# One change at the edges of six stages and in the attention of a two-block kernel

## The reference, cut to what matters

```python
def rwkv_bidir(...):
    kk = k * per_head(k_k)
    kk = kk / jnp.maximum(jnp.sqrt(jnp.sum(kk * kk, axis=-1, keepdims=True)), 1e-12)
    tw = jnp.tanh(xw.astype(f32))
    ...
def banded_attention(q, k, v, max_dist, sinks=None):
    s = ... q k^T * d ** -0.5, masked
    m = max(s.max(axis=-1), sinks)
    p = jnp.exp(s - m[..., None])
    l = p.sum(axis=-1) + jnp.exp(sinks - m)
    o = p @ v
    o = o / l[..., None]
def second_block(...):
    hdn = rmsnorm_2(x, norm_gain)
    ... q, k, v and gates g from hdn @ w_in, norm and rope on q and k
    mixed = concat(o_a * silu(g_a), o_b * silu(g_b))
    return x + mixed @ w_out
```

## Time and profile before

| | |
|---|---|
| median of 3 runs | 2458.24 us (2458.22 to 2469.73) |
| the profiled execution | 2450.08 us, its span 2448.3 us |
| PE busy, its weight loads | 2129.4 us (87%), 1686.8 us (69%) |
| DVE, ACT, POOL busy | 1654.9 (68%), 1268.3 (52%), 675.0 us (28%) |
| mean granted clock of PE | 0.944 of 2.4 GHz |

### The profile page before, as it was taken

The page is one execution under the profiler, slowest core; times in us unless marked ns, Lnnn a source line. Parts: engine busy times, 40 slices in busy tenths (PEclk is TensorE's granted clock), DMA queues, the critical chain, the costliest instruction groups (busy, mean ns, idle before and its releaser), DMA issues. The chain is left out here.

```text
span 2448.3 us, 50472 instructions
## 1 busy us (share of the span) xinstructions
PE 2129.4 (87%) x21006; PEld 1686.8 (69%) x21006; DVE 1654.9 (68%) x2541; ACT 1268.3 (52%) x2327; POOL 675.0 (28%) x472
## 2 busy tenths in 40 slices
PE   5999998499999988973999999999479899778889
PEld 3777787477888743862788888887367788444567
DVE  3665555698888646236899999997367366477941
ACT  5412121476666654434788888886344443365430
POOL 0000011466666501204123322330254545000011
PEclk8999999699999998986999999999799999898999
DMA  7222233333222167326899999997353643200032
GB/s 273 65 56 72 60 83 70 79 68 68 68 69 69 42 225 267 124 113 234 292 394 385 385 388 395 389 386 266 114 190 112 203 111 95 110 1 1 1 104 78
DMA packets 163488, 398.29 MB, mean 163 GB/s; under 512 B 13231, under 2 KB 57405, under 8 KB 163261
## 3 DMA queue, kind: packets, MB, share of 16 engines
q1 hardware_dynamic: 148220, 345.23, 40.3%
q0 software_dynamic: 12224, 44.57, 6.8%
q10 hardware_dynamic: 2816, 5.26, 0.6%
HBM read 348.35 MB, written 46.66 MB: 161 GB/s over the span
## 5 line engine op out<-in xcount | busy, mean ns | idle before, releaser
L1900 DVE TENSOR_TENSOR exp_w_lo<-exp_w,exp_w_hi 128x2048 fp32r<-128x2048 f32 x186 | 414.4, 2290 | 21.9 <-ACT exp_w_hi L1857 21.7
L1857 ACT ACTIVATE exp_w_hi<-exp_w 128x1024 fp32r<-128x1024 f32 x384 | 377.3, 1052 | 66.9 <-PE bank L1819 51.7
L2091 POOL TENSOR_TENSOR w_lo<-mixT,w_hi 128x512 fp32r<-128x512 f32 (+1 forms) x112 | 153.5, 1395 | 175.7 <-ACT w_hi L2167 173.5
L1819 PE MATMUL bank<-exp_w_hi,xsT_lo 128*128 128x512 f32 x512 | 160.8, 396 | 5.7 <-DVE xsT_lo L1904 5.7
L1819 PE MATMUL bank<-exp_w_lo,xsT_hi 128*128 128x512 f32 x512 | 158.8, 392 | 0.0
L1819 PE MATMUL bank<-exp_w_hi,xsT_hi 128*128 128x512 f32 x512 | 158.5, 391 | 0.0
L1787 POOL DMA_INDIRECT moe_rows<-exp_out,idxT x16 | 25.2, 1572 | 437.8 <-DVE exp_out L1959 437.8
L2151 PE MATMUL bank<-w_hi,h_lo 128*128 128x512 f32 (+1 forms) x320 | 123.4, 386 | 1.1 <-POOL w_lo L2091 1.1
L2151 PE MATMUL bank<-w_lo,h_hi 128*128 128x512 f32 (+1 forms) x320 | 120.7, 377 | 0.0
L2151 PE MATMUL bank<-w_hi,h_hi 128*128 128x512 f32 (+1 forms) x320 | 120.3, 376 | 0.0
L1772 POOL DMA_INDIRECT xs<-xn_rows,idxT x16 | 116.0, 7250 | 14.4 <-DVE idxT L1931 5.7
(11 more groups left out here) (372 smaller groups left out, 5797.3 us busy)
## 6 DMA issues: line engine op xcount, KB each, us to landing
exp_w<-in_exp_w_gate_dram SPq DMA_DIRECT2D x64, 1024.0 KB, 9.9
exp_w<-in_exp_w_up_dram SPq DMA_DIRECT2D x64, 1024.0 KB, 10.6
exp_w<-in_exp_w_down_dram SPq DMA_DIRECT2D x64, 1024.0 KB, 7.5
mixT<-in_w_in_dram SPq DMA_DIRECT2D x96, 256.0 KB, 2.9
ada_w_second<-in_ada_w_dram SPq DMA_DIRECT2D x16, 1024.0 KB, 9.5
chunk<-rkv_scratch SPq DMA_DIRECT2D x80, 192.0 KB, 4.0
w_in_ring<-in_w_in_dram SPq DMA_DIRECT2D x26, 512.0 KB, 3.9
rkv_scratch<-work POOLq DMA_DIRECT2D x16, 640.0 KB, 5.9
```

The costliest lines, as they stand in the source:

```text
L1819: mm = pe.matmul(g.ps[bank + q][:, :], lhs[:, kk, :], wide[:, k, q * 512:(q + 1) * 512], start=(kk == 0 and p == 0), stop=(kk == KT - 1 an ...
L1857: last = act.activation(wh[:, n % RH, k, :], w[:, n % RING, k, :], ACT.Copy)
L1900: dve.tensor_tensor(wl[:, n % RH, :, :], w[:, n % RING, :, :], wh[:, n % RH, :, :], ALU.subtract).then_inc(lo_ok, 1)
L2091: pool.tensor_tensor(wl[:, q % SR, 0:width(q)], w[:, q % WR, 0:width(q)], wh[:, q % SR, 0:width(q)], ALU.subtract).then_inc(w_lo, 1)
```

## The change

1. First projection: `order` now ends with `rw` 12, `rw` 13 and the last three convolution tiles. The key sums stand between k steps of the same tile (before k = 2 and k = 6), and DVE reads them (`take_key`) ahead of its weight split. Tanh moves to this stage, and so do the loads of `lora_up`, behind the last weights on SP, into memory that a later stage uses for a row.
2. Both output products: DVE makes the low half of the first token tile, POOL those from the second.
3. Second projection, beginning: a first root on a constant takes the table load, the roots, norms, splits and high and low halves of tiles 0 to 3 are written out in another order, and DVE makes the low parts of weight pieces 1, 3, 5 and 7 (`first_low`), POOL the others.
4. Second projection, later tiles: roots and norms at m - 1 (`START`). The transposes stay.
5. Attention: the window's bias and the sinks are loaded in the stage before; the big bias table behind the first gate. `norm` is gone. One reciprocal for both heads (`invert`), its values spread over 64 features by a product with the identity (`widen`) into the second quarter of the value bank, and `finish` multiplies twice. `soft` is one instruction over up to two banks, for which the eight banks are one tensor (`banks`). With up to four key tiles the heads' transposes alternate between banks 4 and 5.

```diff
-    for i in range(4):
-
+    for i in range(3):
         order += [("rw", 4 + i), ("b", i), ("c", i), ("u", i)]
-    order += [("rw", j) for j in (8, 9, 10, 11, 1, 2, 3, 13, 12)]
+    order += [("rw", j) for j in (7, 8, 9, 10, 11, 1, 2, 3, 12, 13)]
+    order += [("b", 3), ("c", 3), ("u", 3)]
...
+            for d in range(2):
+                sp.dma_start(g.lora_up[0:64, d, :], g.i["w_lora_up"][0, d]).then_inc(g.up_in, 16)
...
+                if n - 2 == order.index(("rw", 12)):
+                    act.wait_ge(mixed, n - 1)
+                    act.activation(g.lora[0:64, :], g.lora[0:64, :], ACT.Tanh)
...
+                if n in HEADS:
+                    take_key(HEADS.index(n))
                 if n + SR < NT:
                     split_lo(n + SR)
...
+                    if n in HEADS and k in (2, 6):
+                        key_sums(HEADS.index(n), (0, 1) if k == 2 else (2,))
...
+            dve.wait_ge(m_hi, 1)
+            for k, rows in ((0, g.yT), (4, g.bT)):
+                last = dve.tensor_tensor(ml[:, 0, k:k + 4, :], rows[:, :, 0:P], mh[:, 0, k:k + 4, :], ALU.subtract)
+            last.then_inc(first_lo, 1)
...
+            def first_low(q):
+                dve.wait_ge(w_hi, q + 1)
+                dve.tensor_tensor(wl[:, q, 0:width(q)], w[:, q % WR, 0:width(q)], wh[:, q, 0:width(q)], ALU.subtract).then_inc(w_lo_first, 1)
...
-                if m in LATER:
-                    final_norm(LATER[m])
-                    second_norm(LATER[m])
+                if m in START:
+                    final_norm(START[m])
+                    second_norm(START[m])
...
             def turn(i):
-                pe.wait_ge(normed, i + 1)
-                if i >= 1:
+                pe.wait_ge(exped, i + 1)
+                if both(i) or i >= 1 and both(i - 1):
                     pe.wait_ge(pcopied_v, i)
                     pe.wait_ge(pcopied_a, i)
+                elif i >= 2:
+                    pe.wait_ge(pcopied_v, i - 1)
+                    pe.wait_ge(pcopied_a, i - 1)
...
+            def widen(p):
+                pe.wait_ge(turned_over, p + 1)
+                if p >= 2:
+                    pe.wait_ge(out_ok, p - 1)
+                for side in range(2):
+                    at = (2 * p + side) % 8
+                    pe.matmul(g.ps[6 + p % 2][64 * side:64 * side + 64, P:2 * P], l[:, at:at + 1].to_broadcast([P, HD]), g.c("ident"),
+                              start=True, stop=True)
...
-                for j, (c0, c1) in enumerate(cuts):
-                    ins = dve.tensor_tensor_reduce(out[:, c0:c1], g.ps[2 * side + j][:, 0:c1 - c0], bias[:, at + c0:at + c1], -1.0,
-                                                   first, ALU.add, ALU.min, m[:, i % 4, j:j + 1])
+                dve.tensor_tensor_reduce(scores(i), g.wide_ps[:, 1024 * side:1024 * side + wide], table, -1.0,
+                                         first, ALU.add, ALU.min, m[:, i % 4:i % 4 + 1]).then_inc(maxed, 1)
...
-                step(dve.reciprocal(l[:, i % 8:i % 8 + 1], l[:, i % 8:i % 8 + 1]))
-                dve.tensor_scalar(pr[:, i % 4, 0:n], pr[:, i % 4, 0:n], l[:, i % 8:i % 8 + 1], None, ALU.mult).then_inc(normed, 1)
...
+                if 1 <= p < NPAIR + 1:
+                    put(2 * p - 2)
+                    invert(p - 1)
                 if p >= 2:
-                    finish(p - 2)
+                    finish(p - 2, 0)
+                if 1 <= p < NPAIR + 1:
+                    put(2 * p - 1)
+                if p >= 2:
+                    finish(p - 2, 1)
```

More of the change, by code:

```diff
@@ L561, in turn_values, with key_sums @@
                 mm.then_inc(vturned, 1)
+            def key_sums(h, thirds):
+                pe.wait_ge(kcopied, h + 1)
+                for q in thirds:
+                    lo, hi = THIRDS[q]
+                    if 3 * h + q >= 2:
+                        pe.wait_ge(khread, 3 * h + q - 1)
+                    pe.matmul(g.ps[6 + q % 2][:, 0:hi - lo], g.c("head"), ksq[:, lo:hi],
+                              start=True, stop=True).then_inc(khead, 1)
             for n in range(NT):
@@ L582, in _ @@
                 mm.then_inc(prod, 1)
-                if n in HEADS:
-                    h = HEADS.index(n)
-                    pe.wait_ge(kcopied, h + 1)
-                    for q, (lo, hi) in enumerate(THIRDS):
-                        if 3 * h + q >= 2:
-                            pe.wait_ge(khread, 3 * h + q - 1)
-                        pe.matmul(g.ps[6 + q % 2][:, 0:hi - lo], g.c("head"), ksq[:, lo:hi],
-                                  start=True, stop=True).then_inc(khead, 1)
                 if n in turns:
@@ L792, in _ @@
         def _(act):
-            act.activation(g.lora[0:64, :], g.lora[0:64, :], ACT.Tanh).then_inc(tanh_ok, 1)
             step = Chain(act, chain_a)
@@ L1576, in _ @@
         def _(pool):
-            for t in range(TT):
+            for t in range(1, TT):
                 pool.wait_ge(m_hi, t + 1)
@@ L2088, in _ @@
             for q, (blk, k) in enumerate(pieces):
+                if q < KT and q % 2:
+                    continue
                 pool.wait_ge(w_hi, q + 1)
@@ L2200, in store @@
                 act.activation(dst[:, :, t * P:(t + 1) * P], g.ps[4 + i % 2][:, 0:k * P].rearrange("p (k t) -> p k t", k=k), ACT.Copy).then_inc(rput, 1)
-            root.n = 0
+            root.n = 1
             act.dma_start(fg, g.i["final_g"].rearrange("(b a n) -> b a n", b=1, a=2).to_broadcast([P, 2, 512])).then_inc(rows_in, 16)
             act.dma_start(ng, g.i["norm_gain_2"].rearrange("b (a n) -> b a n", a=2).to_broadcast([P, 2, 512])).then_inc(rows_in, 16)
-            for i in range(HT + 2):
-                if i < HT:
-                    root(i, 0)
-                if 1 <= i < HT + 1:
-                    root(i - 1, 1)
-                if i < 4:
-                    split(2 * i)
-                    split(2 * i + 1)
-                if i >= 2:
-                    high(i - 2)
+            act.activation(rs[:, 0, 0:1], g.c("eps"), ACT.Sqrt).then_inc(chain_a, 1)
+            split(0)
+            root(0, 0)
+            split(1)
+            root(0, 1)
+            root(1, 0)
+            split(2)
+            high(0)
+            split(3)
+            root(1, 1)
+            split(4)
+            split(5)
+            high(1)
+            root(2, 0)
+            split(6)
+            split(7)
+            root(2, 1)
+            root(3, 0)
+            high(2)
+            root(3, 1)
+            high(3)
             for m, (n, t) in enumerate(tiles):
@@ L2653, in phase_second @@
             g.vb = sb(nc, heads, "vb", [P, TT, BH * HD])
+            g.window = sb(nc, heads, "window_bias", [P, 2 * P])
+            g.sinks = sb(nc, heads, "sinks_sb", [P, AH])
+            (g.win_in,) = sems(nc, signals, "at_window_in")
             phase_second_project(nc, g, signals)
@@ L2683, in build @@
     with ExitStack() as ctx:
-        g.ps = [ctx.enter_context(nc.psum_tensor(f"bank{b}", [P, 512], F32)) for b in range(8)]
+        g.wide_ps = ctx.enter_context(nc.psum_tensor("banks", [P, 8 * 512], F32))
+        g.ps = [g.wide_ps[:, b * 512:(b + 1) * 512] for b in range(8)]
         g.const = sb(nc, ctx, "const", [P, NCONST])
```

154 lines of the change are left out of this document (86 added, 68 removed).

## The result

The changed kernel takes 2366.44 us (median of 4 runs, 2361.78 to 2372.7) beside 2461.64 us for the kernel before: a ratio of 0.9631, interval 0.9601 to 0.9661. In a second, longer comparison it was 2372.67 beside 2452.3 us: 0.9659, interval 0.9632 to 0.9686. By these ratios 84 to 91 us are gone (the medians themselves are 95 and 80 us apart); 74 were forecast. The median lies 18 us under the forecast of 2384 and 2.4 us inside the range of 2364 to 2406, the second one 8.7 us inside. The profiled executions are 2450.1 and 2372.7 us, 77.4 us apart.

A forecast was written before the change was run, and what follows sets the result against it. The kernel was taken as near a PE bound (busy 87%), with gains only where PE waits. Terms 16 + 2 + 2 + 20 + 34.4 = 74.4 us off the 2458.2 us median gave 2384 us, range 2364 to 2406.

The forecast's parts named there:

- First projection and its end: First projection to recurrent stage's start: moved key sums gain 11.5 us, last tile and earlier loads 4.6; together 16 us.
- the 1 us that I gave back at the fourth head: First projection: PE may wait for the first sum's reading where DVE also shifts; 1 us off the gain.
- Output products: First tile of both output products: DVE makes the low half instead of POOL; 2 us, bounds -1 and 5 less 1.
- Second projection's beginning: Start of second projection: roots off the high half's way, odd weight splits on DVE; 2 us, bounds -1 and 5.
- The later norms: Second projection's four later row tiles: earlier roots and norms remove waits and half level; 20 us, bounds 10 and 22.
- (a): Attention: window table and sinks loaded a stage earlier, removing DVE's wait for them; 6 us, bounds 5 and 7.
- (b): Attention's short pairs: gap of 0.76 us goes, widening comes in; 0.39 us on each of 48 pairs, 18.7 us.
- (c): Attention's 16 long pairs: reduction as one instruction, PE decides at 5.63 us; 0.42 us each, 6.7 us.
- (d): Attention's clock: most of the 36 us at half level spared; 3 us of 5.
- the later norms only move their wait: Rival, second projection: ACT's late sigmoid or POOL's splits stop PE at the next block; 15 of 20 us lost, 0.08.
- The rival of a clock that stays low: Rival, attention: half level again for 36 us, kernel at 2399 us; chance 0.14.
- The rival on the other side: Rival, attention: widening ties pairs together, about 1 us new wait per pair, kernel slower at 2500 us; chance 0.02.

The follow-up runs named there:

- sums_at_end: Changed kernel with the key sums back at a tile's end and their reading behind DVE's weight split, new tile order kept; ratio 0.9704 to the kernel before.
- the second trace: Second profiled execution of the unaltered changed kernel, which was also timed again in five rounds against the kernel before: 2372.67 us, ratio 0.9659.
- early_split: Changed kernel with high copy (ACT) and low part (DVE) of later row tiles one tile earlier, ahead of the next roots and norms; ratio 0.9634 to before.
- window_late: Changed kernel with window bias and sinks loaded at the start of attention behind the big bias table, as before; one run, 2377.6 us.
- norm_kept: Changed kernel with probabilities scaled before the transposes as before, no widening; two banks and wide reduction stay; median 2406.3 us, ratio 0.9807 to the kernel before.
- two_parts: Changed kernel with the reduction over more than 512 keys made in two instructions, one bank each; ratio 0.9659 to the kernel before.
- widen_twice: Changed kernel with each widening made twice, same operands and place; ratio 0.9675 to the kernel before.

## Why the prediction was right, and where its terms were off

**The bound.** It was right that the gain lies at PE's waits and in the half level behind some of them, and that in attention PE is next. The main terms were of the right kind. That the profiled sum comes out within 3 us, 74.4 against 77.4, is luck: one term was 10 us too large, others 12 and 4 too small.

**First projection and its end, forecast 16, measured 20.2.** The four waits went whole; the 1 us that I gave back at the fourth head did not come. PE's last product was at 420.81 and is at 406.49, 14.3 us, where I had 11.5; `sums_at_end` shows 14.7 for this step alone. 9.1 are the waits, 3.4 the half level behind two of them, as forecast; the rest I can't assign, and the same product stands anywhere from 404.5 to 406.9 in the traces whose code is the same here. From that product to the recurrent stage's start 13.99 us became 9.05: 4.9, with the 3.4 us at the low-rank weights exact (PE starts 1.22 us behind the barrier, where POOL's memsets begin at 414.32, in place of 4.62). The last 0.9 lies between PE's start there and the first chunk, 17.4 us before and 16.5 after; the chunk loads cost nothing that shows.

**Output products, 2 forecast.** The weight splits of DVE that took up to 2.30 us are all 1.22 to 1.23 us now. POOL begins 2.7 us behind the first of them, and where the two overlap it is now POOL's split that is longer (1.91 us at 943.91, where its next takes 1.27). PE starts 9.2 us behind the last product of the stage before (933.37) where it was 10.2, and 6.6 behind the last value product's start where it was 7.3: 1.7 us.

**Second projection's beginning, 2 forecast, 0.9 measured** (0.5 ahead of the first transposes, 0.4 behind them). Three of DVE's four new splits take 0.69 us, with POOL idle; the fourth, beside one of POOL's, takes 1.79. One norm takes 2.28 us in place of 1.28, also just when POOL splits a weight, and two of POOL's four take 2.06 and 2.07 in place of 1.26. That agrees with the rule of the Trainium skill (SBUF — State Buffer, "Who interferes with whom") on VectorE and GpSimd excluding each other, which I had named as a way to lose this term. What it cost PE is not tested.

```profile
1728.28 2.28 DVE L2296 SCALAR_TENSOR_TENSOR kbT<-qaT,cb_rs,mixT 128x1024 f32<-128x1024 f32 x1
```

```profile
1728.21 1.26 POOL L2111 TENSOR_TENSOR w_lo<-mixT,w_hi 128x512 fp32r<-128x512 f32 x1 [3.10 <-ACT w_hi L2187]
```

```profile
1736.52 1.79 DVE L2307 TENSOR_TENSOR w_lo<-mixT,w_hi 128x512 fp32r<-128x512 f32 x1
```

**The later norms: the step that failed, 20 forecast, 9.8 in this trace.** "The waits of 3.5 us each go: 13.9 us." Only 7.0 went: 2.26, 1.74 and 2.94 us are left. And of the 6.8 us for the half level nothing came in this trace: from its first product to attention the stage had 22 us at 1.2 GHz before and has 23 now. In the second trace 0.63, 1.74 and 2.95 us are left, 11 us run at 1.2 GHz, and 14.3 of the 20 us were won. I had put the one risk at the sigmoid and had looked at the transposes' operand alone. They also need their two banks back, from the low part of the token tile before. This is ACT in the changed kernel, the two squares of tile 5's roots and then the high copy of tile 4 (between them stand two table loads of 1.28 us, a wait for DVE of 1.55, a sigmoid and three weight splits):

```profile
1797.65 1.07 ACT L2200 ACTIVATE kbT<-qaT 128x1024 f32<-128x1024 f32 x1
...
1801.97 1.06 ACT L2200 ACTIVATE kbT<-qaT 128x1024 f32<-128x1024 f32 x1 [1.55 <-DVE qaT L2291]
...
1806.82 1.08 ACT L2210 ACTIVATE later_hi<-banks 128x512 fp32r<-128x512 f32 x2
```

```profile
1809.37 1.17 PE L2147 MATMUL banks<-const,kbT 128*128 128x128 f32 x8 [2.26 <-DVE later_lo L2302]
```

The roots moved ahead of the copy in ACT's queue, the copy ended at 1807.9, DVE's low part behind it at 1809.2, and PE waited. `early_split`, with the copy ahead of the roots, takes both such waits away. The wait of 1.74 stays there; as the trace reads, with no run to test it, it is the norm of tile 6: its first root is early, but DVE works on the rotated tile until 1869.9, and the second root waits for the first norm:

```profile
1869.90 0.15 DVE L2290 RECIPROCAL cb_rs<-cb_rs 128x1 f32<-128x1 f32 x1
```

That is the rival "the later norms only move their wait", half true: the waits moved to the next transposes, by the high copy in ACT's queue, and not to the next block by the sigmoid or POOL's splits. I had given it 0.08. It is also what I had written would prove me wrong: a new wait of over 2 us at a gate tile.

**Attention, 34.4 forecast, 46.8 less 0.7 of the output product measured.** (a) 6 forecast: the first two scores stood 7.29 us apart and now stand 1.22; `window_late` gives 5.1 of it back. (b) 0.39 forecast a short pair, 0.58 measured. The gap of 0.76 us went; the widening I had priced at 0.37 by its busy length, where its pitch, start to start, is 0.27 (and 0.22 for a further two), and the transposes follow the value product after 0.53 us, where in `norm_kept`, without a widening ahead of it, they follow after 0.59. (c) 0.42 forecast a long pair, 0.47 to 0.69 measured. I had let PE decide at 5.63; the chain decides, as `two_parts` (+0.5) and `widen_twice` (0 to 0.13) show, and the chain's 5.54 was right for 5.52. (d) The half level is left at the beginning alone, some 10 us against 36:

```profile
2069.50:2079.50 10.00, 9.56 (x44) 5.14 (x46) 3.91 (x19) 6.51 (x23) 0.00 (x0) 0.51 1.00 379
```

I had taken 3 of 5 us for it, and what it gave is in the pairs' sum. The rival of a clock that stays low did not come. The Trainium skill's rule (TensorE: Matmul & The Clock Gate, "Part 4: PE-mode transpose"), by which transposes count less for the clock, would have made it likelier; in the window of 48 us shown above, with two sets of transposes in every pair, the clock was full throughout. The rival on the other side, pairs tied together by the widening, shows nowhere: PE is never idle ahead of it (busy, mean ns, and idle before, from the groups by line).

```profile
L2481 PE MATMUL banks<-const,row_sum 128*64 128x128 f32 x256 | 28.6, 302 | 0.0
```

**The range.** The profiled sum is nearer than its terms: attention and projection made up what the norms lacked. The medians moved by 80 to 95 us, so that the first of them came out close to the lower end. The rest lies in single executions: that of the kernel before stands 2 to 12 us under its medians in the four comparisons, that of the changed kernel at or 6 us above its own, and the untouched stretches alone spread by 10 us.

## What to carry to other kernels

A wait that has two causes in line (a shared buffer and a step on another engine) pays almost only when both go: 0.13 and 0.18 us alone, 0.58 together. When steps are moved ahead on one engine, list what stands behind them in that queue and which buffer it gives back, not only whether their own result is now in time. Price an added PE product by the pitch of such products, start to start, not by its busy length.

## What the runs showed of the hardware

- Two products that each use 64 columns of the array, one for each half, cost PE no more than one over all 128: from a pair's first transposes to its second it is 1.17 us with the two and 1.18 with the one, and the steady pairs of three and four key tiles take 2.83 and 3.48 us with either. I had expected one to cost half of two.
- A reciprocal on DVE from 128x2 to 128x128 elements takes 0.95 us, where a product of 128x128 takes 0.29 and the reciprocal of 128x2 0.16. The widening by a product on PE is the cheap way.
- DVE's reduction over two banks (128x896) takes 1.02 us to the next, against 1.27 for 512 and 384 in parts: in one instruction the wait of 0.12 us between the parts is saved, and 0.13 more that I put down to a second fixed part.
